# Low keys against high queries only: grouped-query and differential scores as two 64-row tiles of the array

## What is computed

```python
def attend_diff(q, k, v, lam):
    s = jnp.einsum('bqhmd,bkhmd->bhmqk', q, k).astype(jnp.float32) * DIFF_SCALE
    p = jax.nn.softmax(s, axis=-1)
    p = p[:, :, 0] - lam * p[:, :, 1]
    return jnp.einsum('bhqk,bkhv->bqhv', p.astype(v.dtype), v)

def attend_gqa(q, k, v):
    s = jnp.einsum('bqhgd,bkhd->bhgqk', q, k).astype(jnp.float32) * HEAD_SCALE
    p = jax.nn.softmax(s, axis=-1).astype(v.dtype)
    return jnp.einsum('bhgqk,bkhd->bqhgd', p, v)
```

## Time and profile before

| | |
|---|---|
| median of 3 executions | 1669.47 us |
| lowest and highest | 1668.87 and 1670.38 us |
| profiled execution, its own time | 1669.77 us |
| span from first to last instruction in it | 1668.0 us |
| TensorE busy | 1617.9 us, 97% of the span |
| TensorE weight loads busy | 1406.1 us, 84% |
| VectorE, ScalarE, GpSimd busy | 1174.7, 728.2 and 156.7 us |

### The profile page before, as it was taken

One profiled execution on the slowest core, in us unless ns is written; L12 is line 12 of the kernel. 1 busy time (PEld: TensorE's weight loads), 2 busy tenths in 40 slices (PEclk: granted clock), 3 DMA queues, 4 the chain that ended last, 5 costly groups with the idle time before them and its releaser, 6 DMA issues.

```text
span 1668.0 us, 25424 instructions
## 1 busy us (share of the span) xinstructions
PE 1617.9 (97%) x9704; PEld 1406.1 (84%) x9704; DVE 1174.7 (70%) x1994; ACT 728.2 (44%) x1355; POOL 156.7 (9%) x171
## 2 busy tenths in 40 slices
PE   6999999999999999999999999999999899999997
PEld 4999888878789899899898877998877778888885
DVE  5889787684575675666756777844785778777777
ACT  5433466774563122122121237424664665444442
POOL 1000275331000000000000000002441000000000
PEclk9999999999999999999999999999999999999999
DMA  8433430013112433332423322202122132223221
GB/s 345 184 127 127 136 86 20 20 52 127 51 48 105 152 119 134 128 124 101 161 91 150 126 76 102 74 3 48 55 77 102 51 126 102 104 107 112 107 76 51
DMA packets 30263, 170.42 MB, mean 102 GB/s; under 512 B 3920, under 2 KB 6864, under 8 KB 12112
## 3 DMA queue, kind: packets, MB, share of 16 engines
q1 hardware_dynamic: 30160, 169.03, 28.3%
HBM read 156.17 MB, written 2.10 MB: 95 GB/s over the span
## 4 chain that ended last, share of the span: by engine, by line
PE 83%; DVE 9%; ACT 3%; issue 3%; DMA 2%; POOL 0%; SPq 0%; DVEq 0%; ACTq 0%
PE ps L1093 17%; PE ps L1095 17%; PE ps L1094 17%; PE ps L1413 15%; PE ps L1145 3%; PE ps L1266 2%; PE ps L1239 2%; PE ps L1159 2%; PE ps L1179 1%; PE ps L1217 1%; PE ps L1174 1%; PE ps L1227 1%; DMA raw<-in_w_ff 1%; DVE nmax L2984 1%; ACT junk L1820 1%
## 5 line engine op out<-in xcount | busy, mean ns | idle before, releaser
L2917 DVE SCALAR_TENSOR_TENSOR ada_junk<-raw,silu_rows 128x1024 bf16<-128x1024 f32 x160 | 195.4, 1221 | 25.9 <-DMA raw<-in_w_ada_t 23.3
L1789 ACT ACTIVATE whi<-raw 128x2048 fp32r<-128x2048 f32 x48 | 91.7, 1911 | 202.0 <-PE ps L1095 175.0
L1093 PE MATMUL ps<-whi,ahi 128*128 128x256 f32 (+1 forms) x512 | 155.7, 304 | 3.4 <-DVE alo L3452 1.6
L1095 PE MATMUL ps<-whi,alo 128*128 128x256 f32 (+1 forms) x512 | 153.4, 300 | 0.0
L1094 PE MATMUL ps<-wlo,ahi 128*128 128x256 f32 (+1 forms) x512 | 153.3, 299 | 0.0
L1093 PE MATMUL ps<-whi,uhi 128*128 128x512 f32 x384 | 149.9, 390 | 0.3 <-DVE wlo L2490 0.3
L1094 PE MATMUL ps<-wlo,uhi 128*128 128x512 f32 x384 | 149.5, 389 | 0.0
L1095 PE MATMUL ps<-whi,ulo 128*128 128x512 f32 x384 | 149.5, 389 | 0.0
L2490 DVE TENSOR_TENSOR wlo<-raw,whi 128x2048 fp32r<-128x2048 f32 x48 | 109.8, 2288 | 53.9 <-ACT whi L1789 53.6
L1095 PE MATMUL ps<-ahi,wlo 128*128 128x512 f32 (+2 forms) x368 | 138.1, 375 | 0.0
L1093 PE MATMUL ps<-ahi,whi 128*128 128x512 f32 (+1 forms) x336 | 127.6, 380 | 1.8 <-ACT stage L2067 1.4
(11 more groups left out here) (311 smaller groups left out, 3803.2 us busy)
## 6 DMA issues: line engine op xcount, KB each, us to landing
raw<-in_w_ff SPq DMA_DIRECT2D x64, 1024.0 KB, 4.8
raw<-in_w_ada_t SPq DMA_DIRECT2D x40, 1024.0 KB, 4.8
raw<-in_w_in_odd SPq DMA_DIRECT2D x9, 1024.0 KB, 4.8
first_raw<-in_w_ada SPq DMA_DIRECT2D x8, 1024.0 KB, 21.3
raw<-in_w_in_even SPq DMA_DIRECT2D x8, 1024.0 KB, 4.8
h<-in_x SPq DMA_DIRECT2D x4, 1024.0 KB, 7.3
raw<-in_w_out_even SPq DMA_DIRECT2D x4, 1024.0 KB, 6.5
raw<-in_na_bias SPq DMA_DIRECT2D x4, 1024.0 KB, 5.0
```

The costliest lines, as they stand in the source:

```text
L1093: pe.matmul(dst, lhs[0], rhs[0], start=first, stop=False)
L1095: return pe.matmul(dst, lhs[1], rhs[0], start=False, stop=last)
L1789: act.activation(whi[w % 2][:, :, :], raw[r % 2][:, :, :], ACT.Copy).then_inc(s_hi, 1)
L2917: return dve.scalar_tensor_tensor(out=scratch[:, :], in0=weights[:, mt, :], scalar=1.0, in1=silu_rows[:, s, :], op0=ALU.mult, op1=ALU.mult ...
```

## The change

Where a score covers 768 keys, its columns are now laid out as twice 384, one half in each of its two banks. The high keys are still multiplied with the stacked query on all 128 rows, now in two matmuls of 384 columns. The low keys are multiplied with the high part of the query alone, in two matmuls on 64 rows each: keys 0 to 383 on rows 0 to 63 of the array, keys 384 to 767 on rows 64 to 127. For that the high part of a query must be in both halves of the partitions, so the half where it is missing is copied by DMA into new tiles `dq_hi2` (three slots of 256 columns) and `gq_hi2` (two slots). The product of low key with low query is no longer formed. The maximum and the exponential read the two halves of 384 through a view in two pieces. Scores of context tiles over 256 keys, latent attention and neighbourhood attention stay as they were.

```diff
+        dq_hi2 = place("dq_hi2", [P, 3, UW], F32R, B + 9 * KB)
+        gq_hi2 = place("gq_hi2", [P, 2, SEQ], F32R, C + 52 * KB)
...
+        HALF_KEYS = TOK // 2
+        def score_halves(place_):
+            return ps[:, 1024 * place_:1024 * place_ + 1024].rearrange("p (b n) -> p b n", b=2)[:, :, 0:HALF_KEYS]
...
+            def grouped_query_hi(p):
+                if p >= 2:
+                    sp.wait_ge(s_s1, 8 * (p - 1))
+                for m in range(2):
+                    src_rows, dst_rows = slice(64 * m, 64 * m + 64), slice(64 - 64 * m, P - 64 * m)
+                    sp.dma_start(gq_hi2[dst_rows, p % 2, :].bitcast(F32),
+                                 gq2[src_rows, 2 * p + m, :].bitcast(F32)).then_inc(s_gq_hi2[p % 2], 16)
...
+            def diff_query_hi(hd, pair):
+                u = 2 * hd + pair
+                if u >= 3:
+                    sp.wait_ge(s_s, 2 * NT * ((u - 3) // 2) + 4 * ((u - 3) % 2) + 4)
+                cols_ = slice(UW * pair, UW * pair + UW)
+                for m in range(2):
+                    src_rows, dst_rows = slice(64 * m, 64 * m + 64), slice(64 - 64 * m, P - 64 * m)
+                    sp.dma_start(dq_hi2[dst_rows, u % 3, :].bitcast(F32),
+                                 dq2[src_rows, 2 * hd + m, cols_].bitcast(F32)).then_inc(s_dq_hi2[u % 3], 16)
...
                 diff_keys(0)
+                diff_query_hi(0, 0)
+                diff_query_hi(0, 1)
+                diff_query_hi(1, 0)
...
                 diff_keys(1)
+                diff_query_hi(1, 1)
+                diff_query_hi(2, 0)
                 diff_keys(2)
+                diff_query_hi(2, 1)
+                diff_query_hi(3, 0)
...
                 diff_keys(3)
+                diff_query_hi(3, 1)
...
                     if kind == "bias" and r == bias_raw[0]:
...
+                        grouped_query_hi(0)
+                        grouped_query_hi(1)
                         band_moves()
+                    if kind == "bias" and r == bias_raw[2]:
+                        grouped_query_hi(2)
+                        grouped_query_hi(3)
...
+                    if kind == "diff" and t < NTL:
+                        u = 2 * hd + t // 2
+                        pe.wait_ge(s_dq_hi2[u % 3], 32 * (u // 3 + 1))
+                        for half in range(2):
+                            keys = dkeys[:, hd % 2, part, 0, HALF_KEYS * half:HALF_KEYS * half + HALF_KEYS]
+                            pe.matmul(ps[:, c0 + 512 * half:c0 + 512 * half + HALF_KEYS], dq2[:, 2 * hd + part, tcol], keys,
+                                      start=True, stop=False)
+                        for half in range(2):
+                            rows_ = slice(64 * half, 64 * half + 64)
+                            q = (dq2[rows_, 2 * hd + part, tcol] if half == part else
+                                 dq_hi2[rows_, u % 3, P * (t % 2):P * (t % 2) + P])
+                            keys = dkeys[rows_, hd % 2, part, 1, HALF_KEYS * half:HALF_KEYS * half + HALF_KEYS]
+                            last = pe.matmul(ps[:, c0 + 512 * half:c0 + 512 * half + HALF_KEYS], q, keys,
+                                             start=False, stop=True)
+                        last.then_inc(s_s, 1)
+                        return
...
                     if kind == "gqa":
-                        for a, b in ((0, SEQ), (SEQ, TOK)):
-                            for keys in (gkhi, gklo):
-                                last = pe.matmul(ps[:, b0 + a:b0 + b], gq2[:, 2 * p + m, tcol], keys[:, p // 2, a:b],
-                                                 start=keys is gkhi, stop=keys is gklo)
+                        pe.wait_ge(s_gq_hi2[p % 2], 32 * (p // 2 + 1))
...
+                            rows_ = slice(64 * half, 64 * half + 64)
+                            q = gq2[rows_, 2 * p + m, tcol] if half == m else gq_hi2[rows_, p % 2, tcol]
+                            keys = gklo[rows_, p // 2, HALF_KEYS * half:HALF_KEYS * half + HALF_KEYS]
...
+                    if i < N_DIFF and width == TOK:
+                        dst, src = dst.rearrange("p (b n) -> p b n", b=2), score_halves(s % 2)
...
-                        dve.tensor_reduce(nmax1[:, c:c + 1], ps[:, b0:b0 + TOK], AX.X, ALU.max,
+                        dve.tensor_reduce(nmax1[:, c:c + 1], score_halves(i % 2), AX.XY, ALU.max,
```

More of the change, by code:

```diff
@@ L277, in build @@
         s_dkeys = [sem("diff_keys_moved0"), sem("diff_keys_moved1")]
+        s_dq_hi2 = [sem(f"diff_query_hi_moved{i}") for i in range(3)]
         s_krope = [sem("key_rope_rows_moved0"), sem("key_rope_rows_moved1")]
         s_qrope = [sem("query_rope_rows_moved0"), sem("query_rope_rows_moved1")]
+        s_gq_hi2 = [sem(f"grouped_query_hi_moved{i}") for i in range(2)]
         s_band = sem("band_values_moved")
@@ L800, in attention_moves @@
                 sp.wait_ge(s_g, G_QR - NT)
+                for f in range(4):
+                    wait_group_copied(sp, tg_index["in0", 2 + f // 2, f % 2, 0])
                 diff_keys(0)
+                diff_query_hi(0, 0)
+                diff_query_hi(0, 1)
+                diff_query_hi(1, 0)
                 sp.wait_ge(s_g, G_QR)
@@ L821, in straight @@
                     if kind == "bias" and r == bias_raw[0]:
+                        for u in range(2):
+                            for f in range(2):
+                                wait_group_copied(sp, tg_index["in1", u, f, 0])
+                        grouped_query_hi(0)
+                        grouped_query_hi(1)
                         band_moves()
+                    if kind == "bias" and r == bias_raw[2]:
+                        grouped_query_hi(2)
+                        grouped_query_hi(3)
                     if r >= 10:
@@ L1214, in scores @@
                     if kind == "gqa":
-                        for a, b in ((0, SEQ), (SEQ, TOK)):
-                            for keys in (gkhi, gklo):
-                                last = pe.matmul(ps[:, b0 + a:b0 + b], gq2[:, 2 * p + m, tcol], keys[:, p // 2, a:b],
-                                                 start=keys is gkhi, stop=keys is gklo)
+                        pe.wait_ge(s_gq_hi2[p % 2], 32 * (p // 2 + 1))
+                        for half in range(2):
+                            keys = gkhi[:, p // 2, HALF_KEYS * half:HALF_KEYS * half + HALF_KEYS]
+                            pe.matmul(ps[:, b0 + 512 * half:b0 + 512 * half + HALF_KEYS], gq2[:, 2 * p + m, tcol], keys,
+                                      start=True, stop=False)
+                        for half in range(2):
+                            rows_ = slice(64 * half, 64 * half + 64)
+                            q = gq2[rows_, 2 * p + m, tcol] if half == m else gq_hi2[rows_, p % 2, tcol]
+                            keys = gklo[rows_, p // 2, HALF_KEYS * half:HALF_KEYS * half + HALF_KEYS]
+                            last = pe.matmul(ps[:, b0 + 512 * half:b0 + 512 * half + HALF_KEYS], q, keys,
+                                             start=False, stop=True)
                     else:
@@ L2096, in exponentials @@
                         act.wait_ge(s_t, freed)
-                    act.activation(even_probs(i)[part][:, 0:width], ps[:, 1024 * (s % 2):1024 * (s % 2) + width], ACT.Exp,
+                    dst, src = even_probs(i)[part][:, 0:width], ps[:, 1024 * (s % 2):1024 * (s % 2) + width]
+                    if i < N_DIFF and width == TOK:
+                        dst, src = dst.rearrange("p (b n) -> p b n", b=2), score_halves(s % 2)
+                    act.activation(dst, src, ACT.Exp,
                                    bias=nmax[:, s % 4:s % 4 + 1], scale=1.0,
@@ L2163, in exponentials @@
                         b0 = 1024 * (i % 2) + 512 * m
-                        last = act.activation(dst, ps[:, b0:b0 + n], ACT.Exp, bias=nmax1[:, c:c + 1], scale=1.0,
+                        src = ps[:, b0:b0 + n]
+                        if rounds[i][0] == "gqa":
+                            dst, src = dst.rearrange("p (b n) -> p b n", b=2), score_halves(i % 2)
+                        last = act.activation(dst, src, ACT.Exp, bias=nmax1[:, c:c + 1], scale=1.0,
                                               accum_out=rsum1[:, c:c + 1])
@@ L2983, in maximum @@
                     dve.wait_ge(s_s, s + 1)
+                    if i < N_DIFF and width == TOK:
+                        dve.tensor_reduce(nmax[:, s % 4:s % 4 + 1], score_halves(s % 2), AX.XY,
+                                          ALU.max, negate=True).then_inc(s_mx, 1)
+                        return
                     dve.tensor_reduce(nmax[:, s % 4:s % 4 + 1], ps[:, 1024 * (s % 2):1024 * (s % 2) + width], AX.X,
```

## The result

| | before | changed |
|---|---|---|
| median | 1669.82 us (4 executions) | 1680.55 us (4 executions) |
| lowest and highest | 1668.87 and 1670.38 | 1679.45 and 1682.63 |
| ratio, 95% interval | | 1.0066 [1.0051, 1.0081] |
| profiled execution, its span | 1669.77, 1668.0 | 1681.61, 1679.8 |

The change makes the kernel 10.7 us slower. The prediction said 1680.2 us, from 1674 to 1687.

A forecast was written before the change was run, and what follows sets the result against it. TensorE was taken as the bound, busy 97% of the span; 6.2 us in the grouped-query stage plus 4.5 in the differential stage, 10.7 on 1669.77, gave 1680.2 us, range 1674 to 1687.

The forecast's parts named there:

- What bounds it: In both changed stages TensorE's own sequence sets the time; the other engines have room, and the clock explains nothing.
- Grouped-query stage, +6.2 us: 16 pairs of scores at 0.41 us each make 6.5 us on the path, less about 0.3 in holes.
- Streaming and excursion: Each changed score saves 0.17 us of matmul streaming and pays 0.35 to 0.40 for switching to 64-row tiles and back.
- Differential stage, +4.5 us: 32 scores at 0.18 us make 5.8 us, less 1.3 hidden in holes; ends 2.4 and 5.8.
- what holes swallow: TensorE's waits for exponentials in the differential stage absorb 0.15 to 0.2 us at some seven places, 1.3 us.
- Reads in two pieces and the new DMAs, zero: Row maximum and exponential in two pieces, and the new query copies, add no time.
- a few us once: If layer 1's last new query copy came late, TensorE would wait a few us one time.
- No drain: Low-key matmuls start while high-key ones still stream, so only the saving of 11 us remains: 1658.5 us; 7%.
- half-price excursion: At tile-shape changes the drains stand but weight loads are hidden: +0.02 us a score, 1670.7 us; 5%.
- serial halves: The two low-key matmuls of a score stream in turn, another 0.17 us each score, 1691 us; 5%.
- the slow rate: fp32r low-key matmuls on 64 rows run at f32's rate, 0.64 us instead of 0.17, 1710 us; 3%.
- What stays as it was: Everything before 190 us and between the two changed stages should keep its length.

The follow-up runs named there:

- the kernels that share it: Only the grouped-query half of the change applied to the kernel before, 1676.83 us; and the changed kernel with head pair 2's copy issued before the bias loads, 1679.62 us.
- same-rows kernel: Changed kernel with both low-key halves of each score on the same 64 rows: 1690.33 us against 1670.6 for the kernel before, ratio 1.0124.
- mirrored one: Grouped-query scores only, copy early, first score high then low keys, second low then high: 1671.57 us against 1670.1 for the kernel before.
- with the copy early: Changed kernel with low keys on all 128 rows and head pair 2's copy issued before the bias loads: 1671.25 us against 1670.1 for the kernel before.
- grouped-query kernel: Kernel before with only the grouped-query scores changed, differential scores as they were: 1676.83 us against 1670.6, ratio 1.0036.
- with faster scores: Changed kernel with low keys multiplied on all 128 rows, copies not moved: 1676.64 us against 1670.6 for the kernel before, ratio 1.0036.

## Why the prediction was right, point by point

- **What bounds it.** Right: but for 0.2 us of waiting for a copy, the time that the two stages grew by came from TensorE's own sequence.
- **Grouped-query stage, +6.2 us.** Measured 6.06, and 6.26 and 5.89 in the kernels that share it; 0.19 and 0.40 us of the first two are the wait for a copy, so the shape itself cost some 5.9. Per pair it was 0.39 instead of 0.41; the values and second transposes behind the scores took 2.09 us instead of 2.11.
- **Streaming and excursion.** -0.17 and +0.35 to 0.40 a score. Measured from the pair, 0.39 / 2 + 0.17 = 0.37, between the two, and in their parts 0.40 in front of a score and 0.35 in front of transposes, as priced. The same-rows kernel confirmed the first, the mirrored one the second. The neighbourhood scores, a visit of another type, were the right row to take the price from.
- **Differential stage, +4.5 us.** 3.77 and 3.76 were measured. The term that was mis-sized is what holes swallow: 5.8 - 3.8 = 2.0 us and not 1.3, inside the ends given. The trace showed 0.20 and 0.27 us taken at two holes where 0.15 to 0.2 was allowed for each.
- **Reads in two pieces and the new DMAs, zero.** Right in the sum (0.03 and 0.13 us with the copy early), but the step on head pair 2's copy was wrong as reasoned: "near 1170, with their first reader near 1175" took a landing of a few us for granted. It took 7.7 us, and TensorE waited for it 0.19 us once, 0.40 in the grouped-query kernel and 4.63 with faster scores. The prediction had the wait as "a few us once"; what it had not seen is the low clock behind it.
- **The rivals.** No drain falls with the 0.25 and 0.18 us of idle before the loads, the half-price excursion with the pair of 4.72 us where it said 4.4, serial halves and the slow rate with the same-rows kernel. (The slow rate was priced at 0.64 us, which is f32's rate and serial halves at once; side by side it would be 384 / 256 x 0.215 = 0.32 us. Neither is the measured 0.17.) The Trainium skill's "TensorEngine Tiling (Array Packing)", section "Key Properties", has the drain on changing the mode right; the runs put 0.37 us on going in and out.
- **What stays as it was.** "Everything before 190 us" was 1.27 us longer in the profiled execution, with the clock at the start: "the clock explains nothing here" holds for the two stages, but not for the difference between executions. The medians are 10.7 us apart and the stages give 9.8 of them. The sum of the forecast was 10.7 as well; that it was met to 0.1 us is luck, since the differential stage was put 0.7 too high and the wait for the copy at nothing, and some 0.9 us lie outside both stages.

## What to carry to other kernels

Price a change of tile shape before the streaming that it saves: here a visit to 64-row tiles costs 0.37 us on TensorE and two matmuls of 384 columns side by side save 0.17, and two scores sharing one visit came out level; a visit pays only where it replaces clearly more than 0.4 us of streaming. When several uses are put into one visit, look first at whose result it makes late: the wait that follows can be as long as the visit. And where a time misses the expectation by as much as a whole effect, look for a single place in the trace before giving up a theory. A short wait of TensorE need not show as idle: here 0.19 us lay under the modelled end of the records in front, and only the distance between two starts, held against the same distance elsewhere, gave it away.

## What was unexpected of the hardware

- Copies from SBUF to SBUF of 64x512 numbers landed 2.3 to 2.9 us after their issue, but 7.5 to 9.4 us when two loads of 1 MB had been issued within the 1.2 us before them; moved ahead of these loads, the first of the same copies landed after 2.3 us.
- After TensorE had waited 4.4 us, its granted clock was 0.70, 0.50 and 0.94 in three windows of 2 us and 1.00 again after that, which cost some 1.5 us on top.
- A low-key matmul on 64 rows has a record of 0.44 us when it is the first behind the change of shape and of 0.33 when another stood in front of it in the same shape.
- Two fp32r matmuls on 64 rows start 0.003 to 0.004 us apart and take 0.17 us together for 384 columns, the step of the full array; run in turn on the same rows they take 0.17 more: half the rows at the full rate.

Not tried: an order in which the value product stands directly behind the low-key tiles, so that the exit from 64 rows and the entry to 64 columns fall together.
